# Cached pages in two layouts, and inverse norms of keys as a power on GpSimd, in one hybrid decoder layer

## The reference, cut to what matters

```python
def build_keys(c_kv, k_pe, w_uk, k_head_norm):
    k_nope = jnp.einsum('...lc,chd->...lhd', c_kv, w_uk)
    k_rope = jnp.broadcast_to(k_pe[..., None, :], k_nope.shape[:-1] + (QK_ROPE,))
    return rmsnorm(jnp.concatenate([k_nope, k_rope], axis=-1), k_head_norm)

def one_seq(args):                       # one sample sequence
    q_s, ckv_new, kpe_new, pages = args
    ckv = jnp.concatenate([cache_ckv_l[pages].reshape(past, KV_LORA), ckv_new], axis=0)
    kpe = jnp.concatenate([cache_kpe_l[pages].reshape(past, QK_ROPE), kpe_new], axis=0)
    k = build_keys(ckv, kpe, w_uk, k_head_norm)
    return attn_core(q_s, k, ckv, q_pos, k_pos, w_uv)
# attn_core: softmax(q k^T / sqrt(96)) over the positions, times c_kv, times w_uv
```

## Time and profile before

| | us |
|---|---|
| median of 3 runs (lowest, highest) | 1528.22 (1528.05, 1530.12) |
| the profiled execution, its own time | 1529.87 |
| its span in the trace | 1528.0 |
| PE busy | 1513.9 |
| VectorE busy | 1055.5 |
| ScalarE busy | 659.7 |
| GpSimd busy | 448.2 |
| granted TensorE clock, mean share | 0.997 |

### The profile page before, as it was taken

How to read it: one execution, slowest core, us unless ns; L and a number is a source line. 1 busy time by engine, 2 the same in 40 slices (tenths; PEclk the granted TensorE clock), 3 DMA queues, 4 the chain that set the end, 5 groups by cost and what they waited for, 6 DMA issues and landing times.

```text
span 1528.0 us, 31401 instructions
## 1 busy us (share of the span) xinstructions
PE 1513.9 (99%) x11059; PEld 1463.9 (96%) x11059; DVE 1055.5 (69%) x1738; ACT 659.7 (43%) x1247; POOL 448.2 (29%) x463
## 2 busy tenths in 40 slices
PE   8999999999999999999999999999999999999999
PEld 8999999999999999588999999988999999999999
DVE  6999898422269975865877787864659998985000
ACT  6444445322221241364666666662434544444111
POOL 4000002454455743320233333223551000005432
PEclk9999999999999999999999999999999999999999
DMA  6233334232323571002322222312222333332322
GB/s 176 70 97 98 94 90 123 66 95 76 82 75 96 94 119 48 1 1 61 76 67 60 66 63 63 89 56 71 83 82 67 99 96 89 103 95 80 90 76 82
DMA packets 239316, 122.82 MB, mean 80 GB/s; under 512 B 37041, under 2 KB 236146, under 8 KB 239218
## 3 DMA queue, kind: packets, MB, share of 16 engines
q1 hardware_dynamic: 238354, 121.09, 29.6%
q10 hardware_dynamic: 864, 0.48, 0.1%
HBM read 117.95 MB, written 3.58 MB: 80 GB/s over the span
## 4 chain that ended last, share of the span: by engine, by line
PE 67%; issue 21%; POOL 7%; DVE 2%; ACT 2%; DMA 1%; SPq 0%; POOLq 0%; ACTq 0%; DVEq 0%
PE ps L490 29%; PE ps L1506 14%; PE ps L1868 11%; POOL w_lobuf L465 7%; PE ps L1760 1%; PE ps L1631 1%; PE ps L1685 1%; PE ps L1660 1%; PE ps L1799 1%; PE ps L1778 1%; PE ps L1828 1%; PE ps L1779 1%; DMA w_rawbuf<-in_ffn_w_gu 1%; PE ps L476 1%; PE ps L1675 1%
## 5 line engine op out<-in xcount | busy, mean ns | idle before, releaser
L465 POOL TENSOR_TENSOR w_lobuf<-w_rawbuf,w_hibuf 128x256 fp32r<-128x256 f32 (+1 forms) x328 | 316.9, 997 | 798.7 <-ACT w_hibuf L458 798.5
L1506 PE MATMUL ps<-xs,w 128*128 128x288 f32 x3192 | 427.4, 296 | 0.8 <-DVE w L1994 0.8
L1506 PEld LDWEIGHTS ps<-xs,w 128*128 128x128 f32 x3192 | 426.8, 188 | 1.3 <-issue 1.3
L458 ACT ACTIVATE w_hibuf<-w_rawbuf 128x1024 fp32r<-128x1024 f32 (+1 forms) x89 | 104.4, 1172 | 348.1 <-PE ps L490 332.9
L2202 DVE SCALAR_TENSOR_TENSOR xT<-ps,xT 128x576 f32<-128x576 f32 x23 | 17.4, 757 | 202.4 <-PE ps L490 202.4
L1994 DVE TENSOR_TENSOR w<-w_raw,w 128x512 fp32r<-128x512 f32 x228 | 153.5, 688 | 1.0 <-ACT w L1006 0.8
L490 PE MATMUL ps<-a_hi,w_lobuf 128*128 128x288 f32 x682 | 147.5, 297 | 0.0
L490 PE MATMUL ps<-x_hi,w_hibuf 128*128 128x288 f32 x656 | 142.6, 299 | 4.6 <-POOL w_lobuf L465 2.7
L490 PE MATMUL ps<-a_hi,w_hibuf 128*128 128x288 f32 x682 | 147.2, 296 | 0.0
L490 PE MATMUL ps<-a_lo,w_hibuf 128*128 128x288 f32 x682 | 145.4, 294 | 0.0
L490 PE MATMUL ps<-x_lo,w_hibuf 128*128 128x288 f32 x656 | 141.3, 297 | 0.0
(11 more groups left out here) (343 smaller groups left out, 2729.6 us busy)
## 6 DMA issues: line engine op xcount, KB each, us to landing
w_raw<-in_ffn_w_gu SPq DMA_DIRECT2D x76, 256.0 KB, 2.9
up_rows<-in_ffn_w_gu SPq DMA_DIRECT2D x72, 256.0 KB, 3.1
c_nat<-in_cache_ckv SPq DMA_DIRECT2D x128, 128.0 KB, 2.0
w_rawbuf<-in_w_in SPq DMA_DIRECT2D x58, 256.0 KB, 3.2
w_rawbuf<-in_ffn_w_down SPq DMA_DIRECT2D x32, 384.0 KB, 4.1
...
w_rawbuf<-in_ffn_w_gu SPq DMA_DIRECT2D x24, 256.0 KB, 3.4
w_rawbuf<-in_w_out SPq DMA_DIRECT2D x16, 256.0 KB, 3.2
```

The costliest lines, as they stand in the source:

```text
L458: act.activation(w_hibuf[:, r % HIS, 0:size], w_rawbuf[:, r, 0:size], ACT.Copy).then_inc(w_hi_done, 1)
L465: ins = pool.tensor_tensor(w_lobuf[:, r, part], w_rawbuf[:, r, part], w_hibuf[:, r % HIS, part].bitcast(F32), ALU.subtract)
L1506: mm = pe.matmul(ps[:, seven_bank(f, slot), 0:HALF], m, xs[:, slot, n, k, :], start=k == 0 and j == 0, stop=k == KH - 1 and j == 2)
```

## The change

The host now lays the cache out three times: `pages_t` (each page transposed, as 128 rows of 256), `pages_in` (latent rows and rope keys side by side, 288 wide) and `pages_k` (rope keys transposed). SP loads the transposed pages into a ring of 8 slots in SBUF (`c_ring`), the rows into `c_nat` (now 288 wide), and the rope keys of four pages into `kpeT`. It reads four page numbers at a time, then waits for `ct_lo` and issues four ring DMAs, waits for `pe_scored` and issues four rope-key DMAs, waits for `pages_used` and issues four row DMAs. TensorE's page and rope-key transposes and ScalarE's rope-key copies are gone; `cT_hi` and `cT_lo` are made from the ring instead of PSUM. Products of pages go over three pairs of banks (2, 4, 0) instead of two. GpSimd squares the rope keys in place. The reciprocal on VectorE and the root on ScalarE give way to one `pow` with an exponent tile of -0.5 on GpSimd (`key_roots`), first in GpSimd's work of a sequence, and once more behind `sequences`. `c_lo_first` goes; all low parts overwrite their pages. `w_uv`, whose place the ring takes, is reloaded only after the last `ct_lo`. Some small tiles move.

```diff
+        c_nat = place("c_nat", [P, 2, NP, KL + DR], F32, A0)
...
+        RING = 8
+        c_ring = place("c_ring", [P, RING, KL], F32, S3)
+        minus_half = place("minus_half", [P, NP * H], F32, ring_at + 8 * DK * P + 8192 + 8 * (SQ + KN + SQ))
...
+        nat_in = [[sem(f"nat_in{b}{g}") for g in range(NP // 4)] for b in range(2)]
+        ring_in = [sem(f"ring_in{g}") for g in range(2)]
+        kpe_in = [sem(f"kpe_in{g}") for g in range(2)]
+
+        def ring_pair(pp):
+
+            at = (2 * pp + RING // 2) % RING
+            return c_ring[:, at:at + 2, :].rearrange("p t c -> p (t c)")
+
+        ct_hi, ct_lo = sem("ct_hi"), sem("ct_lo")
...
         def page_banks(t):
 
-            return 2 + 2 * (t % 2)
+            return 4 if t == NP - 1 else (2, 4, 0)[t % 3]
+
+        def banks_free(t):
+
+            return {0: -3, 1: 0, 2: -1, NP - 1: NP - 2}.get(t, t - 2)
...
+            def load_ring(g, found):
+
+                for u, page in enumerate(found):
+                    sp.dma_start(c_ring[:, (4 * g + u + RING // 2) % RING, :], pages_t[ds(page, 1), :, :].rearrange("a p c -> (a p) c"))\
+                        .then_inc(ring_in[g % 2], 16)
+
+            def load_rows(b, g, found):
+
+                for u, page in enumerate(found):
+                    sp.dma_start(c_nat[:, b, 4 * g + u, :], pages_in[ds(page, 1), :, :].rearrange("a p c -> (a p) c")).then_inc(nat_in[b][g], 16)
+
+            def load_kpe(g, found):
+
+                for u, page in enumerate(found):
+                    sp.dma_start(kpeT[u * DR:(u + 1) * DR, g % 2, :], pages_k[ds(page, 1), :, :].rearrange("a d t -> (a d) t")).then_inc(kpe_in[g % 2], 16)
+
+            def load_pages(s, b, used=None):
+
                 for g in range(NP // 4):
-                    if used is not None and g == 0:
-                        sp.wait_ge(split_made, split)
-                    elif used is not None:
+                    found = [page_of(s, 4 * g + u) for u in range(4)]
+                    sp.wait_ge(ct_lo, s * PAIRS + (2 * g - 2))
+                    load_ring(g, found)
+                    sp.wait_ge(pe_scored, s * (NP // 4) + (g - 1))
+                    load_kpe(g, found)
+                    if used is not None:
                         sp.wait_ge(pages_used, used + 2 * (g + 1))
-                    for t in range(4 * g, 4 * g + 4):
-                        page = page_of(s, t)
-                        load_page(cache_ckv, c_nat, ckv_in, page, b, t)
-                        load_page(cache_kpe, kpe_nat, kpe_in, page, b, t)
...
             sp.wait_ge(uk_split, 1)
-            for t in (4, 5, 6, 7, 0, 1, 2, 3):
-                load_page(cache_kpe, kpe_nat, kpe_in, page_of(0, t), 0, t)
-            for t in range(8, NP):
-                page = page_of(0, t)
-                if t >= AHEAD:
-                    load_page(cache_ckv, c_nat, ckv_in, page, 0, t)
-                load_page(cache_kpe, kpe_nat, kpe_in, page, 0, t)
+            found = [page_of(0, 4 + u) for u in range(4)]
+            load_ring(1, found)
+            load_kpe(1, found)
+            load_rows(0, 3, [page_of(0, 12 + u) for u in range(4)])
+            for g in (2, 3):
+                found = [page_of(0, 4 * g + u) for u in range(4)]
+                sp.wait_ge(ct_lo, 2 * g - 2)
+                load_ring(g, found)
+                sp.wait_ge(pe_scored, g - 1)
+                load_kpe(g, found)
             sp.wait_ge(prep_mm, 2)
             load_pages(1, 1)
             with sp.Fori(1, NS // 2) as i:
                 for b in range(2):
-                    load_pages(i * 2 + b, b, i * (2 * PAIRS) + (EARLY_PAIRS + PAIRS * (b - 2)), i * (2 * SPLITS) + (SPLITS * (b - 2) + 2))
+                    load_pages(i * 2 + b, b, i * (2 * PAIRS) + (EARLY_PAIRS + PAIRS * (b - 2)))
...
             sp.wait_ge(lat_mm, STACKED)
-            sp.dma_start(w_uv[:, :, :], w["w_uv"][0].rearrange("(k p) h d -> p k (h d)", p=P)).then_inc(late_in, 16)
             for t in range(2):
                 load_merge(t)
+            sp.wait_ge(ct_lo, NS * PAIRS)
+            sp.dma_start(w_uv[:, :, :], w["w_uv"][0].rearrange("(k p) h d -> p k (h d)", p=P)).then_inc(late_in, 16)
             sp.wait_ge(page_mm, NS * NP)
             sp.wait_ge(pe_scored, NS * (NP // 4))
...
+            def key_roots(r):
+
+                pool.wait_ge(kinv_done, r + 1)
+                k = k_inv[:, :, :].rearrange("p t h -> p (t h)")
+                pool.tensor_tensor(k, k, minus_half[:, :], ALU.pow).then_inc(kroot_done, 1)
+
             def squares(s, b, uses, prev, nxt):
 
+                if prev:
+                    key_roots(s - 1)
                 if prev and stacked(s):
                     for j in range(EARLY_PAIRS):
...
-                pool.tensor_tensor(ta[:, 0:NP * DR], k, k, ALU.mult).then_inc(kpe_sq, 1)
+                    pool.wait_ge(nat_in[b][g], uses * 64)
+                k = c_nat[:, b, :, KL:KL + DR]
+                pool.tensor_tensor(k, k, k, ALU.mult).then_inc(kpe_sq, 1)
 
             sequences(pool, squares)
+            key_roots(NS - 1)
             for t in range(1, KD):
                 n = n_merge + t
...
-            def pages_hi(n, b):
-
-                act.wait_ge(ct_tr, n + 1)
-                act.activation(cT_hi[:, b, :], ps[:, b, :], ACT.Copy).then_inc(ct_hi, 1)
+            def pages_hi(s, pp):
+
+                act.wait_ge(ring_in[pp // 2 % 2], (s * 2 + (pp // 4 + 1)) * 64)
+                if not (isinstance(s, int) and s == 0 and pp < 2):
+                    act.wait_ge(page_mm, s * NP + (2 * pp - 2))
+                act.activation(cT_hi[:, pp % 2, :], ring_pair(pp), ACT.Copy).then_inc(ct_hi, 1)
...
-                act.wait_ge(kinv_done, r + 1)
-                act.activation(k_inv[:, :, :], k_inv[:, :, :], ACT.Sqrt).then_inc(kroot_done, 1)
                 act.activation(s_buf[0:TS, b, NP, :], s_new[:, ds(r, 1), :, :].rearrange("p s h q -> p (s h q)"), ACT.Copy).then_inc(new_copied, 1)
...
-            def pair_high(r, b, j):
-
-                act.wait_ge(ct_tr, r * PAIRS + (j + 1))
+            def pair_high(r, b, j, uses):
+
+                act.wait_ge(nat_in[b][j // 2], uses * 64)
                 act.wait_ge(pages_used, r * PAIRS + (j + 1))
-                act.activation(c_hi[j % EARLY_PAIRS][:, :, 0:KL], c_nat[:, b, 2 * j:2 * j + 2, :], ACT.Copy).then_inc(p_done, 1)
...
-            def transpose_pair(s, b, uses, pp):
-
-                n = s * (NP // 2) + pp
-                if pp % 2 == 0:
-                    pe.wait_ge(ckv_in[b][pp // 2], landed_pages(pp // 2, uses))
-                if not (isinstance(s, int) and s == 0 and pp < 2):
-                    pe.wait_ge(ct_lo, n - 1)
-                for u in range(2):
-                    for k in range(2):
-                        c = (2 * u + k) * P
-                        tr = pe.transpose(ps[:, pp % 2, c:c + P], c_nat[:, b, 2 * pp + u, k * P:(k + 1) * P], ident[:, :])
-                tr.then_inc(ct_tr, 1)
-
             def soft_pe(r, b):
...
+            def kpe_scores(s, g):
+
+                pe.wait_ge(kpe_in[g % 2], (s * 2 + (g // 2 + 1)) * 64)
                 if isinstance(s, int) and s == 0 and g == 0:
                     pe.wait_ge(prep_copied, 2)
-                if not (isinstance(s, int) and s == 0 and g == 0):
+                else:
                     pe.wait_ge(scores_read, s * 4 + g)
-                pe.transpose(ps[:, PEB, 4 * HQ:4 * HQ + P], kpe_nat[:, b, 4 * g:4 * g + 4, :].rearrange("p t d -> p (t d)"), ident[:, :])\
-                    .then_inc(pe_tr, 1)
-
-            def kpe_scores(s, g):
-
-                pe.wait_ge(pe_copied, s * 4 + (g + 1))
...
-                        if not (isinstance(s, int) and s == 0 and t < 2):
-                            pe.wait_ge(page_sq, s * NP + (t - 1))
+                        if not (isinstance(s, int) and s == 0 and t < 3):
+                            pe.wait_ge(page_sq, s * NP + banks_free(t))
...
-            def pages_lo(n, b):
-                dve.wait_ge(ct_hi, n + 1)
-                dve.tensor_tensor(cT_lo[:, b, :], ps[:, b, :], cT_hi[:, b, :].bitcast(F32), ALU.subtract).then_inc(ct_lo, 1)
+            def pages_lo(s, pp):
+
+                dve.wait_ge(ct_hi, s * PAIRS + (pp + 1))
+                dve.tensor_tensor(cT_lo[:, pp % 2, :], ring_pair(pp), cT_hi[:, pp % 2, :].bitcast(F32), ALU.subtract).then_inc(ct_lo, 1)
...
                 own(dve.tensor_tensor(k_inv[:, :, :], page_ss[:, :, :], kpe_ss[:, :, None].broadcast_to([P, NP, H]), ALU.add), 1)
                 own(dve.tensor_scalar(k_inv[:, :, :], k_inv[:, :, :], 1.0 / DH, EPS, ALU.mult, ALU.add), 2)
-                dve.reciprocal(k_inv[:, :, :], k_inv[:, :, :]).then_inc(kinv_done, 1)
+                dve.sem_inc(kinv_done, 1)
...
-    return {"x_t": rows.T, "cols_in": np.concatenate([*gains, taps], axis=1)}
+    ckv, kpe = np.asarray(inputs["cache_ckv"])[0], np.asarray(inputs["cache_kpe"])[0]
```

(49 more changed lines are left out.)

72 lines of the change are left out of this document (27 added, 45 removed).

## The result

The changed kernel takes 1680.19 us (median of 4 runs, 1679.39 to 1681.06), the kernel before beside it 1529.17. The ratio is 1.0984, 95% interval 1.0971 to 1.0997: slower by 151 us, where 1523 was forecast and 1538 was the end of the range.

A forecast was written before the change was run, and what follows sets the result against it. TensorE (PE), busy 1513.9 of 1528.0 us, was taken as the bound, with SP's queue pacing after the change. Stage end -8.1 and power at the end +2.8 sum to -5.3 from the 1528.22 median: 1523 us, range 1498 to 1538.

The forecast's parts named there:

- The power: GpSimd's power for the inverse norms: taken as 3 us each, range to 10, covered in the loop but not at the end.
- rival C: Power of 8 us or more stalls VectorE, then ScalarE's squares, then PE; about 1537 us at 10 us; chance 0.1.
- PE busy near 1483 us: Sign that the forecast is right: PE's total busy time in the changed kernel, 1513.9 us before.
- The tail: End of the sample stage: last power delays GpSimd's split of the second merge weights, +2.8 us, range 0 to 10.
- PE's transposes: Page and rope-key transposes leave PE: 31.7 us go, leaving PE 33.3 us a sequence, 8.3 for four pages.
- SP's queue: SP's DMAs and page numbers set the pace: 9.2 us per four pages, 36.8 a sequence; stage ends 8.1 us earlier.
- over the 76: Sign of being wrong: a loop turn of two sequences above 76 us speaks for a slower SP or a long power.
- rival B: SP's queue is slower still as bytes per page double: at 9.7 us a group, 1538 us; chance 0.23.
- Rival A: Page-number reads on SP overlap, a group takes 8.4 us and PE keeps the pace: 1498 us, up to 1508; chance 0.2.
- nothing on the path: ScalarE loses the square root, its table load and four copies a sequence, claimed to leave the critical path unchanged.
- Collisions of VectorE and GpSimd: Each of 8 `cT_lo` may wait some 0.23 us for GpSimd, 1.8 us a sequence, hidden while SP paces.
- Three pairs of banks: PE may run one page further ahead of ScalarE's squares: gives nothing now, only a cushion for stalls.

The follow-up runs named there:

- e2: The kernel before with only the norms changed: one power per sequence on GpSimd in place of reciprocal and root; 1678.8 us, ratio 1.0972.
- e1: The changed kernel without the power: reciprocal on VectorE and root on ScalarE put back, layouts, ring and three pairs of banks kept; 1538.5 us, ratio 1.0057.
- e5: The changed kernel with the old reciprocal and root put back for the last sequence alone; 1657.2 us, ratio 1.0833.
- e6: e1 with only the last of each group's four rope-key DMAs issued after the first two groups, so work is left out; 1530.6 us, ratio 1.0006.
- e11: e6 with `cT_hi` of pair 6 made by ScalarE behind page 9, ahead of the second half of the exponentials; 1519.0 us, ratio 0.9928.
- e13: e1 with ScalarE's two merge-weight splits moved behind pairs 6 and 7, and `cT_hi` of pair 6 made ahead of the exponentials' second half; 1531.6 us, ratio 1.0018.
- e8: e1 with two pairs of banks, 2 and 4 by turns, as in the kernel before; 1536.3 us, ratio 1.0042.

## Why the prediction was wrong, point by point

- **The power: the step that failed.** It was priced at 3 us, from three reciprocals on VectorE, with 10 as the far end. It takes 20.8, and e2 shows that it alone makes the loss. The mechanism was there as rival C, the chain through VectorE, ScalarE and PE, and so was its second place in front of the merge weights. But the term had no row under it, and "ten times the nearest" was no bound: it was the reciprocal of another engine. The cover was mis-sized too: 3 us in the sum and up to 6 in rival C, it is 1.9, for of each 20.8 us PE waits 18.9 (132.2 of the 133.9 in seven long waits).
- **The lower clock behind stalls** was not in the sum: 19 us. Without the power it still costs: "PE busy near 1483 us" was a sign of being right, and e1 has 1499.3, 16 more, of which the two groups of products above make 14.
- **The tail**: +2.8 for the power at the end (0 to 10), measured 23 by e5. Same failed price. The chain ahead of it came later than forecast as well: the merge weights are asked for at 1003 us in e1, not near 990, and the stage ends at 1024.3, not 1006.7.
- **PE's transposes**: 33.3 us a sequence forecast, 33.7 busy in e6. Right.
- **SP's queue**: 9.2 us a group forecast, 8.9 the bare step, 9.54 measured in e1. The loop's own turn was not priced, and the slow DMA instructions too low. One turn of the loop takes 77.1 us (772.34 to 849.48), over the 76 that were to speak for B or C. By the prediction's own 3 us for each 0.1, a group of 9.54 gives 1533, and 1530 without the power's 2.8; e1's 1538.5 is rival B's figure for a group of 9.7. That it is met is luck: what the 9.54 leave open lies in PE's waits for a second bound that stands level with SP's, ScalarE's order (e6, e11), and in the clock behind them.
- **Rival A** (page numbers overlap) falls. The Trainium skill's "DMA: Bandwidth & Descriptors", in its table of measured facts, gives a tensor load a floor of about 600 ns and an unrolling that amortizes it; in e1 four numbers in a row still cost 2.8 us from the end of the row DMAs at 778.49 to the ring at 781.27, and their loads start 0.63 us apart, as one by one before (0.66). The spacing agrees with the 600 ns; the load itself is 0.27 of it. A gain by unrolling doesn't show here, where each load is followed by its own arithmetic and assertion; four loads with nothing between them weren't run.
- **ScalarE "nothing on the path"** was wrong: its busy time left room, its order didn't. PE's old pace had hidden a `cT_hi` queued behind exponentials, worth 4.5 us in e13 and 11.6 in e11.
- **Collisions of VectorE and GpSimd**: 0.23 us per `cT_lo` forecast; the mean went from 684 ns to 884 in e1, 0.20. Right, and the long ones are collisions: 1.52 us for the `cT_lo` at 886.53, which starts while GpSimd makes two `c_lo` from 885.15 to 887.51. All of them, by tile in the kernel before and in e1 (min/median/max ns):

```profile
L2475 DVE TENSOR_TENSOR cT_lo<-ps,cT_hi x64: 627/687/696, 710.1 to 1005.6; 128x512 fp32r<-128x512 f32 x64
```

```profile
L2478 DVE TENSOR_TENSOR cT_lo<-c_ring,cT_hi x64: 628/692/1554, 711.3 to 1016.0; 128x512 fp32r<-128x512 f32 x64
```

- **Three pairs of banks**: nothing, as forecast (e8; not tried with SP's queue relieved).

## What to carry to other kernels

An operation that no row of the trace shows has no upper bound from the rows of another engine; if the time hangs on it, measure it alone first, and until then keep a range that admits a loss of the size of the whole wait. When the busiest engine is relieved, look beyond busy shares: ask of each other engine, in its own order, what stands ahead of the item that the relieved engine wants next, because its old pace was the cover. And two bounds that are almost level hide each other: alone the cures gave 4.5 us and nothing here, together 11. A short wait of the busiest engine can cost twice, once as time and once as clock behind it; count both.
